# A hybrid decoder step on one core: residual through TensorE, a norm inside the dense stage, an embedding product beside the gathers

## The chip, the core and the metric

One Trainium2 chip, one of its cores. The metric is the device time of one execution in microseconds. The kernel is written instruction by instruction: each engine has its own program, and engines and DMAs wait for each other by semaphores that the code names. PE is TensorE, DVE is VectorE, ACT is ScalarE, POOL is GpSimd, SP is SyncE.

## What is computed

One layer of a decoder for 256 prompt tokens and 64 decode tokens (8 x 8), width 2048, all in float32. The part that matters here comes behind the attention:

```python
h = layer_norm(DEEPNORM_ALPHA * h + mixed, ln1_g, ln1_b)
h = layer_norm(DEEPNORM_ALPHA * h + peer_ffn(h, peer_wq, peer_subkeys, peer_u, peer_v), ln2_g, ln2_b)
gate = jax.nn.sigmoid(jnp.einsum('btd,de->bte', h, ple_gate))
return h + gate * jnp.einsum('btp,pd->btd', p_i, ple_proj)
...
def block(args):                      # of peer_ffn
    xt, et, gt = args                 # tokens, their 128 experts of 16384, gates
    u = u_tab[et]
    h = jnp.einsum('nd,nkd->nk', xt, u, preferred_element_type=jnp.float32)
    a = (gt * jax.nn.gelu(h, approximate=False)).astype(v_tab.dtype)
    return jnp.einsum('nk,nkd->nd', a, v_tab[et])
```

`p_i` has 256 columns; the product with `ple_proj` (256 x 2048) is called the embedding product below.

## The kernel before

Tokens lie on partitions in three tiles: tile 0 is decode (64 rows), tiles 1 and 2 are prompt (128 rows each). Large products take their float32 operands apart into a high part (made by ACT) and a low part (made by POOL for weights, by DVE for activations and V), and TensorE does three matmuls for each (`split_mm`, L1343).

- **Projections.** Weights come in pieces of 1 MB (`load_piece`, L340, two slots), of which ACT makes the high part (`hi`, L530), POOL the low part (`low`, L486). Pieces 0 to 79 are the input, output and query projections; 80 to 95 are the gate projection `ple_gate`, four column chunks of four pieces. `token_piece` (L1351) does a piece for the tiles given to it, 12 matmuls a tile.
- **Selection.** DVE picks each prompt token's experts: `select(t, c)` (L1162) for tile t and query chunk c, then `top_experts` (L1143) writes the expert numbers, which lets POOL start gathering. After `top_experts(0, 1)` DVE does `select(2, 1..3)` and `top_experts(1, 2)`, and then the dots.
- **Gathers and dots.** For each prompt tile and each of its 128 expert places POOL issues one indirect DMA that gathers 128 rows of `peer_u` (8 KB each) into a ring of 7 slots (L499 to L505); DVE multiplies it with the tokens and sums (`prompt_dot`, L1196). Among the dots of tile 2 stands the selection for the decode tokens (`after_dot`, L1229).
- **Gate matrix.** Prompt tokens do not gather `peer_v`. Their weights are put into a dense matrix of 256 tokens by 16384 experts: in 64 groups of four tokens, one-hot matrices of the two expert parts are multiplied on PE (`build`, L1595) into four PSUM banks in turn, and copied to SBUF (`build_copy`, by ACT at L707 and DVE at L1223). Groups 0 to 31 (tile 1) run beside the dots of tile 2; groups 32 to 63 behind them. ACT makes the one-hots of the first 32 and the second one-hots of most others (L678); DVE makes the first ones of groups 32 to 63 (L1208).
- **Dense stage.** 256 pieces of `peer_v` (half a MB each, five slots, loaded by SP at L457) are multiplied with the gate matrix, 12 matmuls a piece, into all eight banks (L1630 to L1641). ACT and DVE make the high and low parts. Between them DVE treats the decode tokens, packed on 128 partitions: 64 dots with gathered rows of `peer_u`, then 64 additions of gathered rows of `peer_v` (`decode_op`, L1254), at the pieces that the table `DECODE_AT` (L316 to L319) names; POOL issues a row when one before it is used.
- **Tail.** The tokens, which SP has written to the output tensor at L445 to make room, are read back at L461. DVE adds the sums from PSUM to them (`add_experts`, L1293), norms tile 1, 2 and 0 (`layer_norm`, L1043: statistics, variance, root by ACT, reciprocal, centring L1055, last step L1057), PE transposes them (`transposes`, L1330, banks by `T_LAST`), ACT and DVE make their parts, and the gate projection runs. Pieces 80 and 81 are done for tiles 1 and 2 first and for tile 0 later. Behind each of the pieces 82 to 93 stands one of the twelve parts of the embedding product (`ple_product`, L1666, plain float32). Sigmoid, product and sum per chunk, and four output DMAs follow.

SP's program is one queue: a wait in it holds back all loads behind it. The rest of the key-value cache copies stands between the loads.

## Time and profile before

| | |
|---|---|
| time, median of 3 runs | 2632.95 us (2630.96 to 2636.36) |
| the profiled execution's own time | 2637.14 us |
| its span, first to last instruction | 2635.3 us |
| PE busy | 1812.7 us, 69% |
| DVE busy | 1744.5 us, 66% |
| POOL busy | 1164.1 us, 44% |
| ACT busy | 867.1 us, 33% |
| moved by DMA | 880.83 MB, 334 GB/s over the span |
| PE clock granted, mean | 0.834 of full |

The page also draws the span in 40 slices: PE is busy at 7 to 9 tenths up to slice 13 and from slice 25 on, and nearly idle between; DVE and DMA are at 8 to 10 tenths in that gap. So the kernel has stages with different limits, and a busy share over the span tells of none of them. In a timeline a row is one instruction (or several alike, with their count), with its start and duration; brackets hold the idle time of the engine before it and what ended it. Matmuls are pipelined, and records of neighbours overlap.

### The profile page before, as it was taken

To read this page: it belongs to the slowest core of one execution; us is meant where nothing else is said; L and a number is where in the kernel's file an instruction comes from. 1 tells how busy PE (TensorE), PEld (TensorE's weight loads), DVE (VectorE), ACT (ScalarE), POOL (GpSimd) and SP (SyncE) were. 2 spreads that over 40 slices of the span, in tenths; PEclk is the share of its full clock that TensorE was granted. 3 is DMA by queue.
4 is the path that set the end of the run, shared out by engine and by line. 5 is a ranking of instruction groups with operands and counts; after the bars stand their busy time and mean duration, and the time that the engine had idled before them with its cause. 6 is when DMAs were issued, how large, how long until landed. Compare 5 with 4: busy or idle time off the path is not lost.

```text
span 2635.3 us, 25343 instructions
## 1 busy us (share of the span) xinstructions
PE 1812.7 (69%) x9670; PEld 1473.5 (56%) x9670; DVE 1744.5 (66%) x2409; ACT 867.1 (33%) x1359; POOL 1164.1 (44%) x484
## 2 busy tenths in 40 slices
PE   7998889999979400000120315999999999997698
PEld 6886778778769300000120314777777777775476
DVE  1054232521138899999999998888888999985321
ACT  2223222232222100000560984544444444443232
POOL 3553234335536148888767881122221222320343
PEclk9998899999989755555555557999999999998799
DMA  9997999978899349999999994799999999996345
GB/s 350 350 351 264 377 404 415 393 310 311 334 335 349 136 190 422 422 422 422 410 374 399 421 422 157 278 351 368 361 361 350 340 382 391 385 347 229 127 159 199
DMA packets 131399, 880.83 MB, mean 334 GB/s; under 512 B 18930, under 2 KB 20530, under 8 KB 55508
## 3 DMA queue, kind: packets, MB, share of 16 engines
q1 hardware_dynamic: 75988, 476.60, 47.3%
q0 software_dynamic: 55296, 402.68, 38.1%
q8 instruction: 74, 1.21, 0.2%
q14 instruction: 41, 0.34, 0.0%
HBM read 870.76 MB, written 141.11 MB: 384 GB/s over the span
## 4 chain that ended last, share of the span: by engine, by line
issue 29%; PE 22%; POOL 21%; DVE 16%; DMA 10%; ACT 1%; POOLq 0%; ACTq 0%; DVEq 0%
POOL expert_rows L504 14%; DMA v_raw<-in_peer_v 7%; PE psum L1347 7%; PE psum L1349 7%; PE psum L1348 7%; POOL w_lo L490 6%; DVE expert_rows L1200 5%; DMA expert_rows<-in_peer_u,experts 2%; DVE v_lo L1281 2%; DVE x_tokens L1269 2%; PE psum L1612 1%; ACT v_hi L753 1%; PE psum L1674 1%; DVE expert_rows L1260 1%; DVE chunk_one_hot L1140 1%
## 5 line engine op out<-in xcount | busy, mean ns | idle before, releaser
L504 POOL DMA_INDIRECT expert_rows<-in_peer_u,experts x256 | 523.1, 2043 | 189.0 <-DVE expert_rows L1200 83.3
L1200 DVE SCALAR_TENSOR_TENSOR expert_rows<-expert_rows,x_tokens 128x2048 f32<-128x2048 f32 x256 | 580.7, 2290 | 36.7 <-DMA expert_rows<-in_peer_u,experts 36.0
L490 POOL TENSOR_TENSOR w_lo<-w_raw,w_hi 128x2048 fp32r<-128x2048 f32 x80 | 373.3, 4667 | 500.5 <-ACT w_hi L535 500.5
L1347 PE MATMUL psum<-v_hi,gate_matrix_hi 128*128 128x512 f32 x1024 | 411.6, 402 | 28.9 <-DVE v_lo L1281 28.1
L753 ACT ACTIVATE v_hi<-v_raw 128x1024 fp32r<-128x1024 f32 x256 | 271.2, 1060 | 413.6 <-DMA v_raw<-in_peer_v 331.0
L1348 PE MATMUL psum<-v_lo,gate_matrix_hi 128*128 128x512 f32 x1024 | 405.5, 396 | 0.0
L1349 PE MATMUL psum<-v_hi,gate_matrix_lo 128*128 128x512 f32 x1024 | 405.2, 396 | 0.0
L1281 DVE TENSOR_TENSOR v_lo<-v_raw,v_hi 128x1024 fp32r<-128x1024 f32 x256 | 312.1, 1221 | 98.8 <-ACT v_hi L753 98.2
L535 ACT ACTIVATE w_hi<-w_raw 128x2048 fp32r<-128x2048 f32 x80 | 153.2, 1914 | 396.5 <-PE psum L1349 354.7
L1593 PE MATMUL psum<-identity,dots 128*128 128x128 f32 x2 | 0.9, 460 | 365.2 <-DVE row_max L1206 365.2
L1347 PEld LDWEIGHTS psum<-v_hi,gate_matrix_hi 128*128 128x128 f32 x1024 | 192.6, 188 | 99.3 <-DVE v_lo L1281 27.6
L1612 PE MATMUL psum<-one_hot_first_gated,one_hot_second 128*128 128x128 f32 x384 | 87.0, 400 | 227.2 <-ACT one_hot_first_gated L704 216.3
L512 POOL DMA_INDIRECT expert_rows<-in_peer_u,experts_decode x64 | 95.3, 1489 | 327.8 <-DVE expert_rows L1260 319.8
L1349 PEld LDWEIGHTS psum<-v_hi,gate_matrix_lo 128*128 128x128 f32 x1024 | 192.7, 188 | 47.1
L1348 PEld LDWEIGHTS psum<-v_lo,gate_matrix_hi 128*128 128x128 f32 x1024 | 192.9, 188 | 43.7
L1612 PEld LDWEIGHTS psum<-one_hot_first_gated,one_hot_second 128*128 128x128 f32 x384 | 75.3, 293 | 238.8 <-ACT one_hot_first_gated L704 219.7
L1347 PE MATMUL psum<-act_T_hi,w_hi 128*128 128x320 f32 x640 | 202.9, 317 | 7.0 <-DVE conv_z L870 2.0
L512 POOL DMA_INDIRECT expert_rows<-in_peer_v,experts_decode x64 | 96.2, 1504 | 249.8 <-DVE x_tokens L1269 229.5
L1593 PEld LDWEIGHTS psum<-identity,dots 128*128 128x128 f32 x2 | 0.4, 183 | 365.8 <-DVE row_max L1206 330.1
L1348 PE MATMUL psum<-act_T_lo,w_hi 128*128 128x320 f32 x640 | 199.9, 312 | 0.0
L1349 PE MATMUL psum<-act_T_hi,w_lo 128*128 128x320 f32 x640 | 199.8, 312 | 0.0
L1347 PE MATMUL psum<-w_hi,act_T_hi 128*128 128x512 f32 x480 | 188.9, 394 | 9.0 <-POOL w_lo L490 5.1
(273 smaller groups left out, 3255.1 us busy)
## 6 DMA issues: line engine op xcount, KB each, us to landing
v_raw<-in_peer_v SPq DMA_DIRECT2D x256, 512.0 KB, 7.3
out<-in_state_attn_k SPq DMA_DIRECT2D x64, 1020.0 KB, 9.8
out<-in_state_attn_v SPq DMA_DIRECT2D x64, 1020.0 KB, 10.0
w_raw<-in_w_in SPq DMA_DIRECT2D x48, 1024.0 KB, 7.9
cache_part<-in_k_parts SPq DMA_DIRECT2D x40, 1024.0 KB, 11.6
cache_part<-in_v_parts SPq DMA_DIRECT2D x40, 1024.0 KB, 13.5
w_raw<-in_w_out SPq DMA_DIRECT2D x16, 1024.0 KB, 5.2
w_raw<-in_peer_wq SPq DMA_DIRECT2D x16, 1024.0 KB, 6.3
```

What stands on the lines that cost most here:

```text
L490: nc.gpsimd.tensor_tensor(l_, r_, h_.bitcast(f32), ALU.subtract).then_inc(w_lo_ready, 1)
L504: pool.indirect_dma_start(ring[n % NSLOT][:, :], None, u_tab, bass.IndirectOffsetOnAxis(idx_p[:, n // PAIRS, n % PAIRS:n % PAIRS + 1], 0)) ...
L512: pool.indirect_dma_start(ring[i % DSLOT][:, :], None, u_tab if i < 64 else v_tab, bass.IndirectOffsetOnAxis(idx_d[:, i % 64:i % 64 + 1], ...
L535: A(bufs[1][:, slot, :, :], bufs[0][:, slot, :, :], ACT.Copy).then_inc(w_hi_ready, 1)
L753: A(vhi[m % HS][:, :], vrl[m % RL][:, :], ACT.Copy).then_inc(vh_ok, 1)
L1200: V.scalar_tensor_tensor(out=g, in0=g, scalar=1.0, in1=xt[:, t, :], op0=ALU.mult, op1=ALU.mult, accum_out=hdot[:, t, j:j + 1]).then_inc(u_ ...
L1269: V.scalar_tensor_tensor(out=ydec, in0=g, scalar=hdot[:, 0, i - 64:i - 63], in1=ydec, op0=ALU.mult, op1=ALU.add).then_inc(d_free, 1)
L1281: V.tensor_tensor(vlo[m % RL][:, :], vrl[m % RL][:, :], vhi[m % HS][:, :].bitcast(f32), ALU.subtract).then_inc(vl_d, 1)
L1347: MM(out, lh, rh, start=start, stop=False)
L1348: MM(out, lh, rl, start=False, stop=False)
L1349: return MM(out, ll, rh, start=False, stop=stop)
L1612: m = MM(PS[:, g % 4, j * NK:(j + 1) * NK], second_one_hot(g, j), emov[:, g % 2, j, :], start=True, stop=True)
```

## The change

1. The selections of tile 2 move in between the dots of tile 1: `select(2, 1)`, `(2, 2)`, `(2, 3)` and `top_experts(1, 2)` stand behind dots 8, 24, 40 and 56.
2. The embedding product runs as a whole between the two `part_transposes` on PE, its copies on ACT there too. Its result (`ple_out_early`, on the memory of the projections' weights) is written to the output tensors by SP, and read back into `ple_out` in the tail. The gate matrix, which takes the same memory, waits for that write.
3. The tokens of tiles 1 and 2 are scaled in place by ACT and brought by PE, with the identity, into the banks of the dense sums (`add_tokens`), so that the dense matmuls start with `start=False`. They are not written out and read back any more, and `add_experts` is gone. Tile 1's four banks are 0, 1, 4, 5 and take no builds now: groups 0 to 31 are built in banks 2, 3, 6, 7, groups 32 to 63 in banks 2 and 3 only. V slots 2, 3 and 4 lie elsewhere and are first loaded later.
4. `DECODE_AT`: the 64 dots stand 1.75 pieces apart (before 2), the 64 additions 1.875 (before 1.69), from piece 118 (before 134). The last is at piece 236. The fold of the decode sums, its gain and bias loads and its whole norm stand at pieces 242 to 253.
5. In the tail the statistics and the centring of tiles 1 and 2 read PSUM. The order of the tiles in the last projection is 0, 1, 2: piece 80 for tiles 0 and 1, transposes of tile 2, piece 81 for tiles 0 and 1, then both for tile 2.

```diff
-T_LAST = [(t, g, g + (0 if t else 4)) for t in (1, 2, 0) for g in range(4)]
+OUT_BANKS = ((0, 1, 4, 5), (2, 3, 6, 7))
+T_LAST = [(t, g, OUT_BANKS[t // 2][g]) for t in range(3) for g in range(4)]
+BUILD_BANKS = (2, 3, 6, 7)
...
-        U_AT = {2 * i: i for i in range(64)}
-        W_AT = {134 + (27 * i) // 16: 64 + i for i in range(64)}
-        GELU_AT = 130
+        U_AT = {(7 * i) // 4: i for i in range(64)}
+        W_AT = {118 + (15 * i) // 8: 64 + i for i in range(64)}
+        GELU_AT = 114
+        FOLD_AT = 242
+        ROOT_AT = 250
...
             sp.dma_start(xt[TS:128, 0, :], xt[0:TS, 0, :]).then_inc(pack_in, 16)
-            sp.dma_start(yp_v, xt[:, 1:3, :]).then_inc(spill, 16)
+            sp.wait_ge(w_lo_ready, 80)
+            sp.dma_start(plew[:, :, :], wple_v).then_inc(ple_in, 16)
+            sp.wait_ge(w_used, 80)
+            sp.dma_start(pnat[:, 1:3, :], pp_v).then_inc(ple_in, 16)
+            sp.dma_start(pnat[0:TS, 0, :], ps_v).then_inc(ple_in, 16)
+            sp.wait_ge(ple_ok, 12)
+            sp.dma_start(yp_v, ples[:, 1:3, :]).then_inc(ple_out, 16)
+            sp.dma_start(ys_v, ples[0:TS, 0, :]).then_inc(ple_out, 16)
...
                 if m == 0:
-                    sp.wait_ge(u_free, 128)
+                    sp.wait_ge(x_acc, 1)
                 if m == 2:
-                    sp.wait_ge(u_free, 256)
+                    sp.wait_ge(x_acc, 2)
+                if m == 3:
+                    sp.wait_ge(ab_mm, GROUPS)
                 if m == 4:
-                    sp.wait_ge(ab_mm, GROUPS)
+                    sp.wait_ge(x_acc, 3)
...
-                if m == 250:
+                if m == FOLD_AT:
                     sp.wait_ge(d_free, 128)
-                    sp.dma_start(xt2[0:TS, 0, :], ydec[TS:128, :]).then_inc(fold_in, 16)
-                    sp.dma_start(xt2[:, 1:3, :], yp_v).then_inc(x2_in, 16)
+                    sp.dma_start(xd2[0:TS, :], ydec[TS:128, :]).then_inc(fold_in, 16)
+                    sp.dma_start(ln2[:, 0, :], ln2_g.rearrange("a d -> (a d)").partition_broadcast(128)).then_inc(ln2_in, 16)
+                    sp.dma_start(ln2[:, 1, :], ln2_b.rearrange("a d -> (a d)").partition_broadcast(128)).then_inc(ln2_in, 16)
...
-            for c in range(1, 4):
-                select(2, c)
-            top_experts(1, 2)
...
-            after_dot = {1: {},
+            after_dot = {1: {8: lambda: select(2, 1), 24: lambda: select(2, 2), 40: lambda: select(2, 3),
+                             56: lambda: top_experts(1, 2)},
...
+            decode_norm = {243: decode_sums, 245: lambda: moments(0, decode_parts), 247: lambda: variance(0),
+                           251: decode_centre, 253: lambda: finish(0)}
...
+            sums = [[PS[:, b, :] for b in OUT_BANKS[t]] for t in range(2)]
+            moments(1, sums[0])
+            variance(1)
+            centre(4, 1, sums[0])
+            finish(1)
             transposed_lo(2, 0, 4)
+            moments(2, sums[1])
+            variance(2)
+            transposed_lo(2, 4, 8)
+            centre(5, 2, sums[1])
+            finish(2)
+            transposed_lo(2, 8, 12)
...
+            def add_tokens(t, cs):
+                for c in cs:
+                    m = MM(PS[:, OUT_BANKS[t - 1][c], :], ident[:, :], xt[:, t, c * CW:(c + 1) * CW], start=True, stop=False)
+                return m
...
-                if g >= 4:
-                    if by_dve(g - 4):
...
+                back = 4 if g < GROUPS // 2 + 2 else 2
+                if g >= back:
+                    evacuated(g - back)
...
+                if g == GROUPS // 2 + 3:
+                    pe.wait_ge(x_sc, 2)
+                    add_tokens(2, (2, 3)).then_inc(x_acc, 1)
...
             pe.wait_ge(tl_ready, 32)
-            for k in range(2):
-                token_piece(80 + k, k, 0, W_GATE, (1, 2))
+            token_piece(80, 0, 0, W_GATE, (0, 1))
             pe.wait_ge(ln_ok, 6)
             transposes(2, 8, 12)
+            token_piece(81, 1, 0, W_GATE, (0, 1))
             pe.wait_ge(tl_ready, 36)
             for k in range(2):
-                token_piece(80 + k, k, 0, W_GATE, (0,))
+                token_piece(80 + k, k, 0, W_GATE, (2,))
...
-                if p < 14:
-                    ple_product(p - 2)
```

**On DVE, behind the first table of experts.** `experts<-prompt_expert_part` is the table that lets the gathers start; the rows behind it are before:

```order
L1152 SCALAR_TENSOR_TENSOR experts<-prompt_expert_part 128x128
L1154 MEMSET row_max 128x1
L1155 MEMSET row_max 128x1
L1158 TENSOR_REDUCE cand_top<-gates 128x8
L1159 RECIPROCAL cand_top<-cand_top 128x8
L1160 TENSOR_TENSOR gates<-gates,cand_top 128x128
L1074 MAX chunk_top_values<-second_peer_scores 128x8 x4
L1077 MAX_INDEX chunk_top_keys<-chunk_top_values,second_peer_scores 128x8 x4
L1080 MATCH_REPLACE second_peer_scores<-chunk_top_values,second_peer_scores 128x128 x4
```

and now (line numbers of the changed kernel):

```order
L1178 SCALAR_TENSOR_TENSOR experts<-prompt_expert_part 128x128
...
L1186 TENSOR_TENSOR gates<-gates,cand_top 128x128
L1222 SCALAR_TENSOR_TENSOR expert_rows_98,dots<-expert_rows_98,x_tokens 128x2048
...
L1222 SCALAR_TENSOR_TENSOR expert_rows_99,dots<-expert_rows_99,x_tokens 128x2048
L1100 MAX chunk_top_values<-second_peer_scores 128x8 x4
L1103 MAX_INDEX chunk_top_keys<-chunk_top_values,second_peer_scores 128x8 x4
```

Before, three selections (the first begins at L1074) stand ahead of the first dot; now nine dots (L1222) come first, and the selection behind them.

**On DVE, behind the last low part of the dense stage.** Before, with `x_tokens_again` the tokens read back (the rows behind the first norm's last step repeat for the other tiles):

```order
L1288 TENSOR_TENSOR x_tokens_again<-x_tokens_again,x_tokens 64x2048
L1297 SCALAR_TENSOR_TENSOR x_tokens_again<-x_tokens_again,psum 128x512 x8
L1303 MEMSET row_max 128x1
L1048 BN_STATS ln_stats<-x_tokens_again 128x6 x4
L1050 BN_AGGR ln_mean_var<-ln_stats 128x2
...
L1055 SCALAR_TENSOR_TENSOR x_tokens_again<-x_tokens_again,ln_mean_var,ln_gain_bias 128x2048
L1057 SCALAR_TENSOR_TENSOR x_tokens_again<-x_tokens_again,ln_std,ln_gain_bias 128x2048
```

and now:

```order
L1300 BN_STATS ln_stats<-psum 128x6 x4
L1305 BN_AGGR ln_mean_var<-ln_stats 128x2
...
L1316 SCALAR_TENSOR_TENSOR prompt_out_tokens<-psum,ln_mean_var,ln_gain_bias 128x512 x4
L1320 MEMSET row_max 128x1
L1325 SCALAR_TENSOR_TENSOR prompt_out_tokens<-prompt_out_tokens,ln_std,ln_gain_bias 128x2048
L836 TENSOR_TENSOR out_T_lo<-psum,out_T_hi 128x4x64 x4
L1300 BN_STATS ln_stats<-psum 128x6 x4
```

The additions (L1297) are gone, the statistics and the centring read PSUM, and the low parts of the decode tile (L836) stand directly behind the first prompt tile's norm.

**On PE, from the query projection to the first build.** Before, the transposes of the two tables (L1588) and of the weights (L1593), and then the builds (L1612):

```order
L1563 MATMUL psum<-subkeys_T,peer_queries 64x128 x16
L1588 MATMUL psum<-identity,prompt_expert_part 128x128 x4
L1593 MATMUL psum<-identity,dots 128x128
L1612 MATMUL psum<-one_hot_first_gated,one_hot_second 128x128 x128
L1593 MATMUL psum<-identity,dots 128x128
```

and now:

```order
L1645 MATMUL psum<-identity,prompt_expert_part 128x128 x2
L1689 MATMUL psum<-identity,ple_tokens 128x64 x2
L1689 MATMUL psum<-identity,ple_tokens 128x128 x4
L1698 MATMUL psum<-ple_weights,ple_T 64x512 x2
L1698 MATMUL psum<-ple_weights,ple_T 128x512 x4
...
L1645 MATMUL psum<-identity,prompt_expert_part 128x128 x2
L1650 MATMUL psum<-identity,dots 128x128
L1660 MATMUL psum<-x_tokens,identity 128x512 x4
L1678 MATMUL psum<-one_hot_first_gated,one_hot_second 128x128 x128
```

The embedding product (L1689, L1698) stands between the two tables' transposes, and four products that bring in the scaled tokens (L1660) stand ahead of the first build.

## Rows read from the trace of the kernel before

**Rows 1.** Table of windows: stretch; busy us (instructions) of engines; clock, DMA share, GB/s
```profile
905.00:953.40 48.40, 1.22 (x4) 0.42 (x4) 46.13 (x188) 0.86 (x3) 6.99 (x7) 0.50 0.38 152
1100.00:1250.00 150.00, 0.00 (x0) 0.00 (x0) 137.90 (x119) 0.00 (x0) 129.67 (x61) 0.50 1.01 422
1267.70:1600.60 332.90, 66.89 (x257) 57.20 (x257) 317.04 (x372) 203.63 (x565) 252.28 (x126) 0.50 0.99 403
1600.60:1659.60 59.00, 40.97 (x257) 35.84 (x258) 43.19 (x154) 40.82 (x95) 0.70 (x1) 0.88 0.16 60
1659.60:2031.90 372.30, 365.50 (x1537) 286.97 (x1538) 325.72 (x322) 170.19 (x194) 92.87 (x64) 1.00 0.96 357
2031.90:2367.90 336.00, 321.94 (x1346) 248.79 (x1345) 306.17 (x236) 150.07 (x168) 91.82 (x61) 1.00 0.96 369
2373.47:2387.47 14.00, 14.00 (x62) 11.25 (x61) 7.43 (x8) 6.43 (x7) 0.00 (x0) 1.00 0.58 184
2367.90:2418.90 51.00, 46.73 (x193) 36.89 (x191) 24.53 (x24) 19.37 (x21) 0.00 (x0) 0.97 0.73 261
2418.90:2486.40 67.50, 28.14 (x127) 22.82 (x127) 38.50 (x51) 13.95 (x22) 16.16 (x4) 0.69 0.24 98
2486.40:2626.10 139.70, 139.70 (x552) 103.96 (x552) 20.49 (x18) 34.48 (x34) 59.77 (x13) 0.98 0.53 194
```

**Rows 2.** Chain of work that ended last: start us, us, what
```profile
137.13 4.60 POOL w_lo L490
...
153.45 4.60 POOL w_lo L490
...
1298.45 17.79 DVE expert_rows L1200 x16
```

**Rows 3.** Timeline of POOL: start, duration; in brackets the idle before
```profile
955.94 2.75 POOL L504 DMA_INDIRECT expert_rows<-in_peer_u,experts  x1 [42.12 <-DVE expert_rows L1200]
...
2437.34 11.60 POOL L490 TENSOR_TENSOR gate_w_lo<-gate_w_raw,gate_w_hi 128x2048 fp32r<-128x2048 f32 x2 [81.79 <-ACT gate_w_hi L535]
```

**Rows 4.** Timeline of VectorE, gathers: start us, duration us, line, operation, operands
```profile
910.98 0.20 DVE L1099 CAST chunk_top_keys_f<-chunk_top_keys 128x64 f32<-128x64 uint32 x1
...
926.37 0.20 DVE L1099 CAST chunk_top_keys_f<-chunk_top_keys 128x64 f32<-128x64 uint32 x1
...
953.37 2.29 DVE L1200 SCALAR_TENSOR_TENSOR expert_rows<-expert_rows,x_tokens 128x2048 f32<-128x2048 f32 x1
...
1090.18 2.29 DVE L1200 SCALAR_TENSOR_TENSOR expert_rows<-expert_rows,x_tokens 128x2048 f32<-128x2048 f32 x1 [0.18 <-DMA expert_rows<-in_peer_u,experts]
```

**Rows 5.** Timeline of PE, four places: end of builds, transposes, piece 82, product
```profile
1654.69 1.13 PE L1612 MATMUL psum<-one_hot_first_gated,one_hot_second 128*128 128x128 f32 x8 [0.28 <-issue]
...
2445.29 3.65 PE L1339 MATMUL psum<-identity,x_tokens_again 128*128 128x128 f32 x16 [9.27 <-DVE out_T_lo L810]
...
2486.39 0.79 PE L1347 MATMUL psum<-gate_w_hi,out_T_hi 128*128 128x512 f32 x1 [6.85 <-POOL gate_w_lo L490]
...
2607.88 1.88 PE L1674 MATMUL psum<-ple_weights,ple_T 128*128 128x512 f32 x4
```

**Rows 6.** Timeline of VectorE behind the dense stage
```profile
2418.90 4.99 DVE L1297 SCALAR_TENSOR_TENSOR x_tokens_again<-x_tokens_again,psum 128x512 f32<-128x512 f32 x8 [3.88 <-PE psum L1349]
...
2432.14 2.46 DVE L1048 BATCH_NORM_STATS2 ln_stats<-x_tokens_again 128x6 f32<-128x512 f32 x4
...
2435.68 2.35 DVE L1055 SCALAR_TENSOR_TENSOR x_tokens_again<-x_tokens_again,ln_mean_var,ln_gain_bias 128x2048 f32<-128x2048 f32 x1
2438.07 6.47 DVE L1057 SCALAR_TENSOR_TENSOR x_tokens_again<-x_tokens_again,ln_std,ln_gain_bias 128x2048 f32<-128x2048 f32 x1
...
2471.23 1.42 DVE L810 TENSOR_TENSOR out_T_lo<-psum,out_T_hi 128x256 fp32r<-128x256 f32 x4 [13.74 <-ACT out_T_hi L548]
```

**Rows 7.** Timeline of ACT: second gelu, and one high part
```profile
1600.66 0.31 ACT L666 ACTIVATE dots<-dots 128x128 f32<-128x128 f32 x1 [27.15 <-DVE row_max L1246]
...
2598.21 1.91 ACT L535 ACTIVATE gate_w_hi<-gate_w_raw 128x2048 fp32r<-128x2048 f32 x1 [6.45 <-PE psum L1349]
```

210 lines of the change are left out of this document (121 added, 89 removed).

## The prediction, made before the changed kernel was timed

> **What bounds the kernel now.** I read the table of windows first, because the kernel is a row of stages with different limits, then the timelines at the borders between stages. Shares over the whole span would say nothing here.
>
> [rows 1] is that table. From 905 to 1600.6 us the prompt tokens' expert rows are gathered and dotted; a window inside it shows DMA at 1.01 and 422 GB/s, so a gathered block of 128 rows of 8 KB, 1.049 MB, takes 1.049 / 422 GB/s = 2.485 us. VectorE's dots follow each other by 2.22 us when their rows are there already: 16 records are 8 dots with their accumulator reads, in 17.79 us [rows 2]. So DMA bounds this stage by a small margin, except where VectorE has other work. Ahead of it lies a hole: in 905 to 953.4 the DMA share is 0.38. POOL has issued seven gathers, which fill the ring of seven slots, and waits 42.12 us for the first dot [rows 3]. That dot starts at 953.37, because VectorE first does three selections, 15.39 us apart [rows 4].
>
> From 1600.6 to 1659.6 the second half of the gate matrix is built by TensorE, ScalarE and VectorE in a tight loop. From 1659.6 to 2418.9 TensorE bounds the dense product: a clean stretch does 5 pieces in 14.00 us, 2.80 each, at the full granted clock. The stage takes 759.3 us for 256 pieces, 42.5 above 716.8: 13.9 in pieces 0 to 127, 22.4 in 128 to 239, 6.2 in the last 16 (each stretch of [rows 1] less its pieces times 2.80).
>
> The tail is two things. From 2418.9 to 2486.4 VectorE's norms and the transposes stand in front of TensorE, whose clock is granted at 0.69. From 2486.4 to 2626.1 TensorE does the last fourteen pieces of the gate projection, with a part of the embedding product behind each of the first twelve.
>
> **Part 1: the embedding product leaves the last projection.** One of its twelve parts is four records over 1.88 us [rows 5]; the records overlap their neighbours, so I count 1.72 of it as TensorE's own. Is it TensorE that bounds a piece once the product is gone? A piece of the first projection has the same 36 matmuls and the same high and low parts, and two of them take 153.45 - 137.13 = 16.32 us [rows 2], 8.16 each. The stretch of 139.7 us is 14 x 8.16 + 12 x 1.72 and 4.8 for the ramp and the joins. So 12 x 1.72 = **-20.6 us**. In its new place TensorE is idle and ScalarE is busy 0.86 of 48.4 us [rows 1]. At the clock of 0.50 its 24 products take 24 x 0.86 x 2 = 41 us and are over by about 950. SP's queue is empty of other work there. The 2.6 MB written are 6 us of DMA, in a stretch where part 3 finds DMA idle. The read back of as much lies in a tail that moves under half of the 422 GB/s. Cost: nothing.
>
> **Part 2: the norms.** Before, VectorE's first instruction after the last dense matmul stands at 2418.90 [rows 6] and piece 82 starts at 2486.39 [rows 5]: 67.5 us. After, counted from that first instruction: four statistics of the sums in PSUM take 2.5 (as four from SBUF do), and 1.1 us later (2434.60 to 2435.68 in [rows 6]: variance, ScalarE's root, reciprocal) the centring starts, at 3.6. Four centrings from PSUM at 0.62 (eight such instructions took 4.99) end at 6.1. The norm's last step I take at 6.47 us, not at 2.35: the one of 2438.07 [rows 6] lay under POOL's low parts [rows 3], and ScalarE makes their high parts at the same point now. It ends at 12.6. Decode's low parts (1.4), the second tile's statistics (2.5) and variance (0.5) take VectorE to 17.0; beside them the first tile's sixteen transposes (3.65, [rows 5]) end at 16.8, and its low parts at 19.5. TensorE runs piece 80 for two tiles (5.6, and 1.5 for a slow start) to 26.7, the last tile's transposes to 30.4, piece 81 for two tiles to 36.0, and both pieces for the third tile to 41.6. The high part (1.91, [rows 7]) and low part (4.60) of piece 82 wait for piece 80 to be through, at 38.8: piece 82 starts at 45.5. Saved: 67.5 - 45.5 = **-22 us**. The 5.0 us of additions and the decode tile's norm, some 8 us, are in it. The decode norm now stands at pieces 243 to 253, 9.6 us of VectorE work where VectorE is busy 24.5 of 51.0 us [rows 1]: hidden by TensorE's pieces, and without that cover 9.6 us dearer.
>
> The Trainium skill (SBUF — State Buffer, "Who interferes with whom") says that VectorE and GpSimd share a port pair under an exclusive lock: a VectorE instruction with two SBUF inputs holds or waits for it, and issue order decides who waits. By that rule the 6.47 us were 2.35 of work behind a low part; if the step came first, by the 0.7 us that lie between the two, the tail would give 26 and the sum 2581. The trace agrees with a wait of that length in [rows 3, 6] and does not show the other order.
>
> **Part 3: selections between the dots.** The first dot comes at about 910.5 instead of 953.37. Nine dots at DMA's 2.485 end at 932.9; three selections (46.2), 48 dots at 2.22 (106.6) and 1.3 for the second table of experts bring dot 57 to 1087.0, against 1090.18 before [rows 4]: -3. But its ring is full now. Before, the full ring at the first dot let 57 dots pass in 136.8 us, 4.8 less than DMA's pace of 141.6. Together -8; a count of all 256 rows by the same rules gives -12. I take **-10 us**. It is far from 43, since VectorE, not DMA, bounds the first 57 dots: the wait for VectorE is cut up, not removed. Bounds: 0, and -33 (all that DMA stood idle).
>
> **Part 4: the scaled tokens through TensorE, and the build.** Scaling a tile is about 1.9 us of ScalarE; the first lies in its chain of one-hots, which ends 27.15 us before it is needed [rows 7], the second beside VectorE's first one-hots. Four products of 512 columns at 0.86, 7 us at the half clock, go ahead of the first build and under ScalarE's first one-hots. In the second half two products come into a loop where TensorE is busy 1.13 us a group of matmuls [rows 5]: +1.7. Two banks instead of four make a build wait for the copy of the group two before it, which in the last sixteen groups ScalarE does behind a one-hot: half a group on some six of them, +3. The last two products lie beside the last copy and the first V piece. **+5 us**, bounds 0 and 12.
>
> **Part 5: the dense stage.** Decode rows come every 1.75 pieces (before 2), then every 1.875 (before 1.69). With 0.524 MB a piece and 1.049 MB a row, the demand at 2.80 us a piece was 375 GB/s and then 409; it becomes 401, then 387. The stalls were 0.109 and 0.200 us a piece; on the line between them 401 gives 0.18 and 387 gives 0.14. 112 x 0.18 + 120 x 0.14 = 37, and 6 at the end, where again 2.5 MB go ahead of V pieces: 43 against 42.5. **0 us**. Bounds: -11 (0.109 everywhere) and +19 (0.2 everywhere, and the decode norm bare).
>
> **The sum**: -20.6 - 22 - 10 + 5 + 0 = -47.6. The profiled execution took 2637.14 us (span 2635.3), 4.2 above the median of 2632.95; the sum puts it at 2589.5, and the median at 2585.3.
>
> **Rivals.** (a) *The dense stage pays for the closer rows.* For it: 401 GB/s are asked for where 357 were moved. Against: 409 were asked for later, at 0.2 us a piece. +19: 2604. (b) *The gathers gain their whole hole*, if the selections slip into VectorE's waits for rows: -33 for -10, 2562. Against it: 57 dots and three selections are 173 us of VectorE work, their rows 142. (c) *The last projection does not reach 8.16*, because the chain of load, high and low part sets the piece once the product is gone: +10, 2595. The first projection speaks against it. (d) *Slower than before.* Late rows open gaps in the dense stage and TensorE's clock is granted at its lower level, 1.2 instead of 2.4 GHz; a piece then takes up to 5.6 us, +2.8. It decides from 17 such pieces on; 35 of them are +98, 2683. The last 16 pieces, with 6 us of gaps, took the clock to 0.97 only, and the 1.00 of the rest speaks against it. (e) *The gathers gain nothing*, if the product's copies on ScalarE or its DMAs hold up the second table of experts or the rows: +10, 2595.
>
> **How the numbers follow.** My forecast has 0.66, (a) 0.12, (b) 0.06, (c) 0.08, (e) 0.05, (d) 0.03. The forecast's own terms spread it by about 10 each way. The range goes down to 2567, part of the way to (b), and up to 2604 for (a). About 0.2% (5 us) is what a measurement can tell from no change. All but (d) are faster by more; 0.01 of (d) and 0.01 of bad ends together land within it: faster 0.95, same 0.02, slower 0.03.
>
> **What would show it.** First dot near 911, dot 57 near 1087; last dot near 1591; 64 us from there to the first dense matmul; 759 for the dense stage; 45.5 from VectorE's first instruction behind it to piece 82; then 119 us of TensorE. The forecast is wrong if the dense stage is over 775, or if pieces of the last projection stay above 9 us.

## The result, and where the time went

Over four runs of each the changed kernel took **2572.51 us** (2562.90 to 2576.15) against 2632.73 us for the kernel before: a ratio of **0.9759, 95% interval 0.9741 to 0.9777**, or 60.2 us less. The forecast for the median was 2585.3 us, 47.6 less, with a range from 2567 to 2604. A second set of runs gave 2576.69 us and a ratio of 0.9764 (0.9723 to 0.9805).

The profiled execution took 2572.92 us with a span of 2571.1. The table of windows of the changed kernel, cut at the same events as [rows 1] (stretch; length; busy us of PE, PEld, VectorE, ScalarE, POOL; granted clock, DMA share, GB/s):

```profile
906.70:1592.50 685.80, 97.81 (x323) 67.41 (x322) 652.18 (x815) 215.96 (x585) 520.72 (x259) 0.52 0.97 399
1592.50:1655.10 62.60, 45.64 (x266) 39.22 (x266) 42.90 (x155) 42.70 (x96) 0.81 (x1) 0.83 0.14 50
1655.10:2034.00 378.90, 360.78 (x1547) 287.24 (x1548) 343.67 (x333) 171.77 (x195) 88.59 (x70) 1.00 0.97 370
2034.00:2354.00 320.00, 310.94 (x1344) 249.87 (x1343) 290.09 (x227) 148.71 (x168) 79.87 (x55) 1.00 0.97 367
2354.00:2402.10 48.10, 43.63 (x185) 35.35 (x183) 29.55 (x32) 18.93 (x22) 0.00 (x0) 0.96 0.65 239
2402.10:2445.80 43.70, 26.64 (x122) 22.15 (x121) 25.63 (x39) 13.71 (x18) 15.68 (x4) 0.77 0.37 138
2445.80:2561.80 116.00, 116.00 (x504) 95.62 (x504) 19.05 (x18) 28.72 (x22) 59.55 (x13) 0.99 0.62 229
```

Three things stand out against [rows 1]. The stretch that began at 905 with a DMA share of 0.38 is no stretch of its own any more: from the first gather to the last dot the mean share is 0.97 (0.95 before). It is not even: it is 0.97 in the first 46.7 us, but 0.87 from 953.4 to 1100, where the kernel before had 0.97. Part of the hole has moved behind the first dots. The stretch of the norms is 43.7 us instead of 67.5, and the last one 116.0 instead of 139.7, with 504 matmuls instead of 552: the 48 of the embedding product are gone. And the first half of the dense stage shows **PE busy 360.78 us for 1547 matmuls**, where the kernel before had 365.50 for 1537. The same matmuls have become cheaper, and no part of the change does that on purpose.

The timelines give the borders exactly. Both kernels measured from start to start of the named instructions:

| stretch | before | after | change | forecast |
|---|---|---|---|---|
| span's start to the first gather | 904.99 | 906.67 | +1.7 | 0 |
| first gather to last dot | 693.21 | 683.53 | -9.7 | -10 |
| last dot to first dense matmul | 61.41 | 64.88 | +3.5 | +5 |
| first to last dense matmul | 758.86 | 746.63 | **-12.2** | 0 |
| last dense matmul to piece 82 | 67.92 | 44.03 | -23.9 | -22 |
| piece 82 to the last matmul | 139.35 | 115.77 | -23.6 | -20.6 |
| last matmul to the end | 9.6 | 9.6 | 0.0 | 0 |

The sum is -64.2 between two profiled executions, against -47.6. A good 12 of the 16.6 us that the forecast missed lie in the dense stage, for which it had forecast nothing.

Two matmuls of the same kind in the timeline of PE in the changed kernel, twelve records (one piece) apart in a stretch without a stall (start, duration):

```profile
2339.80 0.39 PE L1404 MATMUL psum<-v_hi,gate_matrix_hi 128*128 128x512 f32 x1
...
2342.52 0.39 PE L1404 MATMUL psum<-v_hi,gate_matrix_hi 128*128 128x512 f32 x1
```

A piece is 2.72 us, where the clean stretch of [rows 1] has five pieces in 14.00, 2.80 each. At a granted clock of 1.00 in both, a matmul follows the last by 0.2267 instead of 0.2333 us. Over 256 pieces that is 20.5 us, of which stalls took back 8: they grew from 42 to 50 us.

### The profile page after: what moved, and what is told of

Its sections match the earlier page's. It is cut to its first block, busy times and chain, and to the rows that moved or that the text cites. A ratio compares the mean times of both kernels' runs of the same rounds, so it can differ in the third digit from the quotient of the medians.

```text
span 2571.1 us, 25379 instructions
## 1 busy us (share of the span) xinstructions
PE 1804.6 (70%) x9686; PEld 1480.7 (58%) x9686; DVE 1733.0 (67%) x2408; ACT 872.7 (34%) x1361; POOL 1138.8 (44%) x484
## 4 chain that ended last, share of the span: by engine, by line
PE 46%; DVE 23%; POOL 12%; DMA 11%; issue 6%; ACT 2%; SPq 0%; ACTq 0%; DVEq 0%; POOLq 0%
PE psum L1404 14%; PE psum L1406 13%; PE psum L1405 13%; POOL expert_rows L523 11%; DVE expert_rows L1222 9%; DMA v_raw<-in_peer_v 7%; DVE v_lo L1348 2%; DMA cache_part<-in_k_parts 2%; DMA expert_rows<-in_peer_u,experts 2%; DVE expert_rows L1283 2%; PE psum L1558 1%; DVE x_tokens L1292 1%; PE psum L1523 1%; ACT v_hi L793 1%; PE psum L1678 1%
## 5 line engine op out<-in xcount | busy, mean ns | idle before, releaser
L1222 DVE SCALAR_TENSOR_TENSOR expert_rows<-expert_rows,x_tokens 128x2048 f32<-128x2048 f32 x256 | 577.8, 2289 | 30.7 <-DMA expert_rows<-in_peer_u,experts 29.7
L523 POOL DMA_INDIRECT expert_rows<-in_peer_u,experts x256 | 514.7, 2011 | 187.7 <-DVE expert_rows L1222 81.4
L1404 PE MATMUL psum<-v_hi,gate_matrix_hi 128*128 128x512 f32 x1024 | 405.9, 396 | 33.5 <-DVE v_lo L1348 33.1
L1405 PE MATMUL psum<-v_lo,gate_matrix_hi 128*128 128x512 f32 x1024 | 399.7, 390 | 0.0
L1406 PE MATMUL psum<-v_hi,gate_matrix_lo 128*128 128x512 f32 x1024 | 399.5, 390 | 0.0
L531 POOL DMA_INDIRECT expert_rows<-in_peer_u,experts_decode x64 | 82.9, 1296 | 304.1 <-DVE expert_rows L1283 296.1
L1405 PE MATMUL psum<-w_lo,act_T_hi 128*128 128x512 f32 x480 | 188.5, 393 | 0.0
L1406 PE MATMUL psum<-w_hi,act_T_lo 128*128 128x512 f32 x480 | 188.4, 393 | 0.0
```

The costliest lines, as they stand in the source:

```text
L523: pool.indirect_dma_start(ring[n % NSLOT][:, :], None, u_tab, bass.IndirectOffsetOnAxis(idx_p[:, n // PAIRS, n % PAIRS:n % PAIRS + 1], 0)) ...
L531: pool.indirect_dma_start(ring[i % DSLOT][:, :], None, u_tab if i < 64 else v_tab, bass.IndirectOffsetOnAxis(idx_d[:, i % 64:i % 64 + 1], ...
L1222: V.scalar_tensor_tensor(out=g, in0=g, scalar=1.0, in1=xt[:, t, :], op0=ALU.mult, op1=ALU.mult, accum_out=hdot[:, t, j:j + 1]).then_inc(u_ ...
L1404: MM(out, lh, rh, start=start, stop=False)
L1405: MM(out, lh, rl, start=False, stop=False)
L1406: return MM(out, ll, rh, start=False, stop=stop)
```

## What the experiments were to decide

The new statistics tile `ln2_mean_var` takes 32 bytes ahead of `gate_matrix_hi` and `gate_matrix_lo`, the two tiles that every dense matmul reads. The high tile starts at 222592 instead of 222560, the low one at 225664 instead of 225632. Theory: the start sets the pace. Rivals: the new table of decode rows, or the shape of the stage around the matmuls. Beyond that each term of the sum was to be isolated, because two terms that came out near their forecast may have done so by chance.

## Experiments on the dense stage

**The kernel before, with 32 bytes ahead of the two tiles.**

```diff
+    off[0] += 32
     ghs = small("gate_matrix_hi", [128, ST, 2 * 128], f32r, 4)
     gls = small("gate_matrix_lo", [128, ST, 2 * 128], f32r, 4)
```

> The kernel before with 32 unused bytes ahead of the two small tiles gate_matrix_hi and gate_matrix_lo, which start 32 bytes off a multiple of 64 there and on one in the changed kernel; nothing else differs. In the dense stage a piece without a stall takes 2.80 us before and 2.72 in the changed kernel. Theory A (the tiles' start address sets it): 2.72 us here, 256 x 0.08 = 20 us less, of which more stalls take back up to 8: 2613 to 2620 us. Theory B (it comes from matmuls that add to sums already in the banks, or from the V slots' places, or from the row table): 2.80 us and no change, 2633 us.

Measured: 2629.48 us, ratio 0.9972 (0.9952 to 0.9991), a piece 2.72 us. The whole dense stage in its table of windows:

```profile
1659.80:2412.10 752.30, 719.99 (x3072) 571.03 (x3072) 656.04 (x580) 338.79 (x383) 187.14 (x125) 1.00 0.94 359
```

With nothing else touched (no other tile lies behind these two) the pace of the changed kernel is there: its cause is the place of the tiles. But the time fell by 7 us and not by 20. PE is busy 719.99 us and the stage takes 752.30. Above 256 clean pieces the stage has 56 us of stalls, where the kernel before had 42.

**The changed kernel, with the same 32 bytes**, so that the tiles start at 222624 and 225696.

```diff
+    off[0] += 32
     ghs = small("gate_matrix_hi", [128, ST, 2 * 128], f32r, 4)
```

> The changed kernel with the same 32 bytes ahead of gate_matrix_hi, which puts both tiles where they are off a multiple of 64, as before. Theory A: a piece without a stall takes 2.80 us again, and the time rises by 12 to 20 us, to 2585 to 2592. Theory B: 2.72 us and no change, 2572 us.

Measured: 2579.46 us, ratio 0.9795 (0.9771 to 0.9820), a piece 2.80 us again. The time rose by less than the 12 to 20 us expected.

```profile
1651.90:2407.20 755.30, 728.86 (x3072) 572.53 (x3072) 664.06 (x591) 339.48 (x384) 167.97 (x125) 1.00 0.94 356
```

**The changed kernel, with the 32 bytes ahead of the low tile alone.**

```diff
     ghs = small("gate_matrix_hi", [128, ST, 2 * 128], f32r, 4)
+    off[0] += 32
     gls = small("gate_matrix_lo", [128, ST, 2 * 128], f32r, 4)
```

> The changed kernel with the 32 bytes between the two tiles, so that only gate_matrix_lo is off a multiple of 64. It is the stationary operand of one matmul in three. If the stationary operand's address costs each matmul that loads it (theory A1), a piece takes 2.72 + 0.08 / 3 = 2.75 us and the time rises by 4 to 7 us; if VectorE's or ScalarE's writes beside it are what costs (A2), it may be anything from 0 to 20 us.

Measured: 2583.34 us, ratio 0.9818 (0.9794 to 0.9843), a piece 2.80 us. Only one matmul in three reads the low tile, and yet the piece lost all it had gained. The mean intervals between starts, over all of the stage that ran without a pause, show how: 0.2326 us from the first matmul to the second, both of which read the high tile, 0.2381 to the third, which reads the low one, and 0.2289 to the next first. In the changed kernel the three are 0.2275, 0.2275 and 0.2276. Reading the displaced tile costs most, and the interval between the two matmuls that do not read it has grown as well.

**The changed kernel, with the tiles 64 bytes up** (222656), to tell whether a start that is 32 past a multiple of 64 was the point.

```diff
+    off[0] += 64
     ghs = small("gate_matrix_hi", [128, ST, 2 * 128], f32r, 4)
```

> The changed kernel with the gate matrix's two tiles moved up by 64 bytes, so that their start stays a multiple of 64; it is the control to the move by 32. Theory A (what slows the dense matmuls is a start that is 32 past a multiple of 64): 2.72 us a piece, time as the changed kernel's, 2570 to 2578. Theory B (any move away from the one address, or the one tile's distance to others, sets it): 2.80 us a piece, 2579 or more.

Measured: 2584.54 us, ratio 0.9812 (0.9792 to 0.9833), a piece 2.80 us.

```profile
1653.80:2408.20 754.40, 732.17 (x3072) 574.29 (x3072) 663.56 (x591) 340.30 (x384) 167.37 (x125) 1.00 0.94 357
```

So no multiple of 64 decides: my reading after the first three runs fell here.

**The tiles 128 bytes up** (222720), together with an edit of the tail that is told below.

```diff
+    off[0] += 128
     ghs = small("gate_matrix_hi", [128, ST, 2 * 128], f32r, 4)
```

> The changed kernel with ScalarE's order in the tail turned as in the run before of that name, and with the gate matrix's two tiles moved up by 128 bytes, which changes nothing else. The high tile's start was 222592 in the changed kernel (2.72 us a piece of the dense stage), 222560 and 222624 (2.80) with 32 bytes less or more, and 222656 with 64 more (2.80), so it is no multiple of 64 that decides. Theory A (a multiple of 128 decides; 222592 is one, 222656 is none, 222720 is the next): 2.72 us a piece, piece 82 again 39 to 40 us behind VectorE's first instruction of the tail, and the whole as the run with the turned order, ratio to the kernel before 0.975 to 0.978. Theory B (the one address or the distance to other tiles decides): 2.80 us a piece and 7 to 10 us more, ratio 0.979 to 0.981.

Measured: 2574.87 us, ratio 0.9761 (0.9737 to 0.9784); a piece 2.78 to 2.80 us.

```profile
1659.50:2414.70 755.20, 729.78 (x3072) 576.75 (x3072) 664.29 (x591) 340.04 (x384) 164.51 (x125) 0.99 0.93 357
```

A multiple of 128 does not decide either. (A start 128 past a multiple of 256, or a distance to other tiles, is not ruled out.) What stands is narrower: of six placements one, 222592 with 225664, gives 2.72 us, in both kernels and in every version of them that kept it; the five others give 2.78 to 2.80. Why that one, the runs do not say.

At the slow pace this run was expected at a ratio of 0.979 to 0.981. It has 0.9761, where the same tail with the tiles at the fast place has 0.9762 (below). Between these two the pace makes no difference in time that can be measured; the other three moved versions, at 0.9795, 0.9812 and 0.9818, are 8 to 16 us behind the changed kernel.

**The changed kernel, with the decode table of the kernel before.**

```diff
-        U_AT = {(7 * i) // 4: i for i in range(64)}
-        W_AT = {118 + (15 * i) // 8: 64 + i for i in range(64)}
+        U_AT = {2 * i: i for i in range(64)}
+        W_AT = {134 + (27 * i) // 16: 64 + i for i in range(64)}
...
-        GELU_AT = 114
+        GELU_AT = 130
```

> The changed kernel with the decode table of before (dots each 2 pieces, additions each 1.69 from piece 134, gelu at 130). The dense stage of the changed kernel stalls 50 us over 256 pieces of 2.72. Theory of the prediction (the tables cost the same, stalls follow the bytes asked for on one line): the same within 4 us, 2572. Rival (the additions at 1.69 stall most, the new table is what gives the dense stage part of its gain): 8 to 16 us slower, 2580 to 2588, and the excess in pieces 134 to 240.

Measured: 2580.97 us, ratio 0.9808 (0.9785 to 0.9832). Its profiled execution, 2568.20 us, is the fastest of its four; there a piece is 2.72 us and the stage from first to last matmul 745.9, so the table is not what made the pieces faster. By the ratios the old table is 0.0044 to 0.0049 worse, 12 us; the profile shows no place for that, and the new table was not measured in the same set of runs. Whether the table gives anything stays open.

**The changed kernel unchanged, a second time**, beside the next three.

> The changed kernel as it is, run again beside the kernel before and beside the three below, because its time against a version of it with the old table of decode rows is to be read on one chip. Theory A (the 2572.5 us are the kernel's): 2568 to 2577, ratio to before 0.974 to 0.978, dense stage 745 to 748 at 2.72 us a piece. Theory B (the first measurement was a lucky one, and the two tables are the same): about 2580, ratio 0.980.

Measured: 2576.69 us (2570.03 to 2583.65). In its profiled execution, 2581.93 us, the dense stage takes 755.0 us at the same 2.72 a piece, where the first one took 746.6. **One execution's dense stage is uncertain by some 8 us**, and the term "-12.2" of the table above is partly that. Taken together (first to last dense matmul, one profiled execution each):

| | a piece | dense stage, us | mean |
|---|---|---|---|
| kernel before and three variants (below) | 2.80 | 758.9, 752.0, 753.4, 756.2 | 755.1 |
| kernel before, 32 bytes | 2.72 | 752.0 | 752.0 |
| changed kernel moved, four variants | 2.78 to 2.80 | 755.0, 756.7, 754.2, 754.9 | 755.2 |
| changed kernel, twice, and three variants | 2.72 | 746.6, 755.0, 748.5, 749.2, 745.9 | 749.2 |

At an equal pace the stage is the same in both kernels, 755.1 and 755.2 us, between executions that scatter by several us: the closer decode rows cost nothing that shows. The faster matmuls are worth 3 to 6 us of the stage by these means, not 20.5. Where did the rest go? One limit is DMA: its share is 0.97 in the two long windows of the changed kernel (0.96 before), and the chain of work that ended last goes, in this stage, again and again through loads of V (start, us):

```profile
1944.23 10.29 DMA v_raw<-in_peer_v
2016.08 8.91 DMA v_raw<-in_peer_v
2042.65 7.77 DMA v_raw<-in_peer_v
2070.28 8.98 DMA v_raw<-in_peer_v
2090.89 8.64 DMA v_raw<-in_peer_v
2149.04 10.32 DMA v_raw<-in_peer_v
```

The pieces of V and the decode rows alone are 268 MB (256 of 0.524 and 128 of 1.049 MB); at the 369 GB/s of these windows they take 727 us, an estimate that leaves a faster TensorE little room.

But VectorE is in the loop too, and the pauses end with it. It makes the low part of every piece and does the decode tokens' work between; by the table of windows it is busy 663.31 of the stage's 747.0 us, 2.59 us a piece. One pause of the changed kernel, piece 44, in the timelines of ScalarE, VectorE and PE:

```profile
1780.43 1.06 ACT L793 ACTIVATE v_hi<-v_raw 128x1024 fp32r<-128x1024 f32 x1 [0.22 <-DMA v_raw<-in_peer_v]
...
1781.02 2.28 DVE L1283 SCALAR_TENSOR_TENSOR expert_rows<-expert_rows,x_tokens 128x2048 f32<-128x2048 f32 x1
...
1783.23 0.61 DVE L1346 TENSOR_TENSOR gate_matrix_lo<-gate_matrix,gate_matrix_hi 128x256 fp32r<-128x256 f32 x1
...
1783.76 1.22 DVE L1348 TENSOR_TENSOR v_lo<-v_raw,v_hi 128x1024 fp32r<-128x1024 f32 x1
...
1785.12 0.47 PE L1404 MATMUL psum<-v_hi,gate_matrix_hi 128*128 128x512 f32 x1 [0.94 <-DVE v_lo L1348]
```

The high part was ready at 1781.49, and VectorE, at work without a pause since 1776.53, began the low part at 1783.76. Counted so over the stage, the pauses of over 0.05 us between pieces are 40 us in the changed kernel, and 29 of them stand before pieces whose high part had been ready for over 0.15 us; before the rest the high part itself came late. In the kernel before it is 20 of 34. Most of these unbroken runs of VectorE begin with a low part that had waited for its load, so the two limits cannot be told apart from this. What is shown is that TensorE, the loads into five slots, ScalarE and VectorE stand in one loop with little slack anywhere. Which of DMA's rate, the five slots and VectorE's work takes back the faster matmuls, no run separates: a version with a sixth slot, or with the decode work off VectorE, was not tried.

## Experiments on the gathers and the build

**The changed kernel, with its selections ahead of the dots again.**

```diff
+            for c in range(1, 4):
+                select(2, c)
+            top_experts(1, 2)
...
-            after_dot = {1: {8: lambda: select(2, 1), 24: lambda: select(2, 2), 40: lambda: select(2, 3),
-                             56: lambda: top_experts(1, 2)},
+            after_dot = {1: {},
```

> The changed kernel with its three selections of the second tile of tokens and the second table of experts put back ahead of the prompt tokens' dots, nothing else. Theory A (the move of the selections alone gives the stage of the dots its 8 us, and nothing beside): the first dot near 955, dot 57 near 1092, the last dot 8 to 10 us later than 1590.2, the whole 2580 to 2584. Theory B (the stage is bound by DMA further on, and what the move gave at its start is lost to it later, so that the 8 us come from somewhere else): last dot within 3 us of 1590.2, the whole within 3 us of the changed kernel. Theory C (the whole hole of 43 us counts): last dot after 1620.

Measured: 2580.16 us, ratio 0.9784 (0.9751 to 0.9817). Its POOL and VectorE timelines, first gather and last dot:

```profile
906.24 1.08 POOL L523 DMA_INDIRECT expert_rows<-in_peer_u,experts  x1 [30.69 <-DVE row_max L1180]
```

```profile
1595.52 2.29 DVE L1225 SCALAR_TENSOR_TENSOR expert_rows<-expert_rows,x_tokens 128x2048 f32<-128x2048 f32 x1
```

The stage takes 689.3 us: 5.8 more than 683.5, and 3.9 less than the 693.2 of the kernel before. The move of the selections is worth 5.8 us, not 9.7, and less than the 8 to 10 expected here. The four profiles of the kernel before and its variants with nothing edited in this stage have 692.4 to 693.5 us, the eight of the changed kernel and its variants 682.4 to 683.9, so both differences are clear of the scatter. Side by side, this version and the kernel before run alike up to dot 128 but for 0.9 us, and part by 2.6 us between dots 128 and 144. In the kernel before that stretch of VectorE's timeline reads:

```profile
1273.28 2.29 DVE L1200 SCALAR_TENSOR_TENSOR expert_rows<-expert_rows,x_tokens 128x2048 f32<-128x2048 f32 x1 [0.76 <-DMA expert_rows<-in_peer_u,experts]
1277.06 2.29 DVE L1200 SCALAR_TENSOR_TENSOR expert_rows<-expert_rows,x_tokens 128x2048 f32<-128x2048 f32 x1 [1.47 <-DMA expert_rows<-in_peer_u,experts]
1280.17 2.29 DVE L1200 SCALAR_TENSOR_TENSOR expert_rows<-expert_rows,x_tokens 128x2048 f32<-128x2048 f32 x1 [0.81 <-DMA expert_rows<-in_peer_u,experts]
```

Rows come 3 to 4 us apart instead of 2.49. Just ahead SP had issued two loads of V, which waited for dot 128; in the changed kernel they wait for the products that bring in the tokens scaled by ScalarE, and go 16.7 us later (SP's timeline, the kernel before, then the changed kernel):

```profile
1267.56 0.81 SPq L457 DMA_DIRECT2D v_raw<-in_peer_v  x2
```

```profile
1284.28 0.82 SPq L479 DMA_DIRECT2D v_raw<-in_peer_v  x2
```

**The kernel before, with these two loads behind dot 138.**

```diff
-                    sp.wait_ge(u_free, 128)
+                    sp.wait_ge(u_free, 138)
```

> The kernel before, with the loads of the first two pieces of V issued behind dot 138 and not behind dot 128 of the prompt tokens; in the changed kernel they wait for the scaling of the tokens, which falls there as well. Theory A (at dot 128 rows are bound by DMA, and the two loads, 1.05 MB, put 2.5 us ahead of the next rows; ten dots on VectorE is busy with the decode selections and they cost nothing): from the first gather to the last dot 690.4 to 691 us instead of 693.2, the whole 2 to 3 us down. Theory B (the loads cost the same wherever they stand): 693 again; the 3.9 us that the changed kernel gains there beside its selections come from elsewhere.

Measured: 2631.01 us, ratio 0.9985 (0.9966 to 1.0003), which as a time is no proof. The stage, read from its timelines, is: first gather at 904.62, last dot at

```profile
1594.78 2.29 DVE L1200 SCALAR_TENSOR_TENSOR expert_rows<-expert_rows,x_tokens 128x2048 f32<-128x2048 f32 x1 [0.17 <-DMA expert_rows<-in_peer_u,experts]
```

That is 690.2 us, 3.0 less than 693.2. But this execution is 1.0 ahead at dot 128 already, where nothing was edited. What the edit does stands behind it: dots 128 to 144 take 43.7 us instead of 46.3, as they do in the changed kernel (43.7), and 46.3 in the three other variants of the kernel before, which leave the loads where they were. The same bytes cost 2.6 us where rows are bound by DMA, and nothing 29 us later (1296.89), where VectorE does decode selections between its dots. So of the stage's 9.7 us, 5.8 are the selections and 2.6 V's first loads; the remaining 1.3 are within the scatter, for the profile of the kernel before is 0.5 to 1.0 behind its four variants at dot 128.

**The kernel before, with the second half of the builds over two banks.**

```diff
+        def build_bank(g):
+            return g % 4 if g < GROUPS // 2 else g % 2
...
+                back = 4 if g < GROUPS // 2 + 2 else 2
+                if g >= back:
...
-                    m = MM(PS[:, g % 4, j * NK:(j + 1) * NK], second_one_hot(g, j), emov[:, g % 2, j, :], start=True, stop=True)
+                    m = MM(PS[:, build_bank(g), j * NK:(j + 1) * NK], second_one_hot(g, j), emov[:, g % 2, j, :], start=True, stop=True)
```

> The kernel before with the gate matrix's second half built over two banks of PSUM instead of four, as the change does it, and nothing else. Theory A (a build waits for the copy of the group two ahead of it): from the last dot to the first dense matmul 64 to 65 us instead of 61.4, and the whole 3 us up. Theory B (ScalarE and VectorE set the pace and two banks are enough): within 1 us of 61.4. Theory C (every group waits): 67 or more.

Measured: 2641.61 us, ratio 1.0013 (0.9992 to 1.0034). From the last dot (1602.23) to the first dense matmul (1666.00) it takes 63.8 us instead of 61.4: **+2.4**, which would leave 1.1 of the 3.5 for the two products of the scaled tokens in the loop. Neither is exact: this stretch takes 61.4 to 62.9 us in the kernel before and its three variants without this edit, and 64.5 to 66.2 in the changed kernel and its variants.

## Experiments on the tail

**The kernel before, without the embedding product**: the twelve parts behind pieces 84 to 95 and their copies are left out, and VectorE multiplies the gate by other data of the same shape, so the output is another.

```diff
-                if p >= 4:
-                    ple_copy(p - 4)
...
-                dve.wait_ge(ple_ok, 3 * c + 3)
...
-                    m = V.tensor_tensor(gsig[0:r, t, :], gsig[0:r, t, :], pleo[0:r, t, cc], ALU.mult)
+                    m = V.tensor_tensor(gsig[0:r, t, :], gsig[0:r, t, :], plew[0:r, 0, cc], ALU.mult)
...
-                if p < 14:
-                    ple_product(p - 2)
```

> The kernel before without the embedding product: the twelve parts that stand behind pieces 84 to 95, their copies by ScalarE and VectorE's wait for them are gone, and the gate is multiplied by the layer norm's weights in its place, so that VectorE's instruction keeps its shape; the output is another. Theory A (each part is 1.72 us of TensorE's own, as the prediction has it): the last stretch falls from 139.7 us by 20.6, its pieces take 8.16 each, the whole comes to 2610 to 2614 beside 2633. Theory B (the new tail's gain of 23.7 in this stretch is the product alone): 139.7 falls by 23 or more, to 116. Theory C (the product lay partly in waits that remain): the fall is under 15.

Measured: 2615.65 us, ratio 0.9923 (0.9902 to 0.9944). The start of piece 82 and the last matmul in PE's timeline:

```profile
2486.53 0.80 PE L1344 MATMUL psum<-gate_w_hi,out_T_hi 128*128 128x512 f32 x1 [6.85 <-POOL gate_w_lo L490]
...
2603.32 0.39 PE L1346 MATMUL psum<-gate_w_hi,out_T_lo 128*128 128x512 f32 x1
```

116.8 us instead of 139.35: **22.6 us for twelve parts, 1.88 each**, which is the full record of [rows 5] and not the 1.72 that I counted.

**The changed kernel, with piece 80's high part behind VectorE's norm step.** In the changed kernel VectorE's timeline behind the dense stage is:

```profile
2402.14 2.49 DVE L1300 BATCH_NORM_STATS2 ln_stats<-psum 128x6 f32<-128x512 f32 x4 [5.84 <-PE psum L1406]
...
2405.71 2.73 DVE L1316 SCALAR_TENSOR_TENSOR prompt_out_tokens<-psum,ln_mean_var,ln_gain_bias 128x512 f32<-128x512 f32 x4
2408.48 5.55 DVE L1325 SCALAR_TENSOR_TENSOR prompt_out_tokens<-prompt_out_tokens,ln_std,ln_gain_bias 128x2048 f32<-128x2048 f32 x1
...
2423.62 2.35 DVE L1325 SCALAR_TENSOR_TENSOR prompt_out_tokens<-prompt_out_tokens,ln_std,ln_gain_bias 128x2048 f32<-128x2048 f32 x1
```

and POOL's:

```profile
2407.36 11.06 POOL L509 TENSOR_TENSOR gate_w_lo<-gate_w_raw,gate_w_hi 128x2048 fp32r<-128x2048 f32 x2 [79.77 <-ACT gate_w_hi L554]
```

The same instruction takes 5.55 us under the low parts and 2.35 without. POOL had begun 1.1 us earlier, and the chain of waits puts the border between its two low parts at 2411.85: from 2408.48 that is 3.37 us, and the remaining 2.18 are about the instruction itself. The second low part, behind the step, then took 6.57 us:

```profile
2411.85 6.57 POOL gate_w_lo L509
```

```diff
+            transposed_hi(2, 0, 4)
+            act.wait_ge(ln_ok, 5)
...
+            transposed_hi(2, 4, 8)
...
-            transposed_hi(2, 0, 8)
```

> The changed kernel with one order of ScalarE's turned in the tail: it makes the first half of the second tile's high parts, then waits for VectorE's last norm step of the first prompt tile, and only then makes piece 80's high part, whose low part GpSimd takes up. No work is added or taken away. In the changed kernel that step of VectorE took 5.55 us under GpSimd's low parts, and 2.35 us without them elsewhere. Theory A (two engines share a lock, and whoever issues first holds it): the step takes 2.35 us, piece 82 starts 40 to 41 us after VectorE's first instruction of the tail instead of 43.6, the whole is 3 us under the changed kernel, 2569 to 2574 on a chip where that takes 2572 to 2577. Theory B (the step is slowed by DMA or PSUM traffic and not by GpSimd): it still takes over 4.5 us and the time is unchanged. Theory C (the low part of piece 80 or 81 comes too late now): the step is short, but TensorE waits at piece 80, 81 or 82 for it, and the time is unchanged or worse.

Measured: 2572.59 us, ratio 0.9762 (0.9743 to 0.9781). The timelines of this version, VectorE:

```profile
2400.53 2.49 DVE L1302 BATCH_NORM_STATS2 ln_stats<-psum 128x6 f32<-128x512 f32 x4 [5.84 <-PE psum L1408]
...
2406.87 2.35 DVE L1327 SCALAR_TENSOR_TENSOR prompt_out_tokens<-prompt_out_tokens,ln_std,ln_gain_bias 128x2048 f32<-128x2048 f32 x1
...
2418.86 3.73 DVE L1327 SCALAR_TENSOR_TENSOR prompt_out_tokens<-prompt_out_tokens,ln_std,ln_gain_bias 128x2048 f32<-128x2048 f32 x1
```

POOL:

```profile
2411.34 9.10 POOL L509 TENSOR_TENSOR gate_w_lo<-gate_w_raw,gate_w_hi 128x2048 fp32r<-128x2048 f32 x2 [84.88 <-ACT gate_w_hi L554]
```

and PE, piece 82:

```profile
2439.73 0.80 PE L1406 MATMUL psum<-gate_w_hi,out_T_hi 128*128 128x512 f32 x1 [3.93 <-POOL gate_w_lo L509]
```

The step is 2.35 us now, and the low parts, which no such step interrupts until they are through, take 9.10 for two instead of 11.06. The second tile's step begins at 2418.86, 1.58 us before they end (2420.44), and takes 3.73. Whoever came first held the other up, in either direction: the steps at 2408.48 and 2418.86 waited for a low part under way, and the second low part of the changed kernel, behind a step, took 6.57 us where two undisturbed ones take 9.10. The Trainium skill (SBUF — State Buffer, "Who interferes with whom") describes it so, and this trace now agrees with it in both orders. Piece 82 starts 39.2 us behind VectorE's first instruction instead of 43.6 (40 to 41 was expected). That is **4.4 us less tail, but not a measurably faster kernel**: 0.9762 beside 0.9759 and 0.9764, with intervals of 0.2 to 0.4% each way. The run with the tiles 128 bytes up holds the same edit, with 40.4 us from VectorE's first instruction (2414.88) to piece 82 (2455.26), and the ratio of 0.9761 already given. A gain of 4.4 us is under what these runs can tell by time alone, and no version tried here is measurably better than the changed kernel.

## Why the prediction was right, and what was off

**Part 1, the product (-20.6; measured -23.6).** The mechanism stands: pieces take 8.16 us without it, and its new place costs nothing (its last copy by ScalarE is at 933.67 us; 950 was forecast). The price was mis-sized. I took 1.72 of the 1.88 us, reasoning that the records overlap their neighbours; alone it measured 1.88, 1.9 us in all. The last 1.0 is the ramp: piece 82 takes 9.91 us in the changed kernel, from its first matmul to that of the next piece, and 10.93 in the kernel before without the product. TensorE idled less ahead of it (clock 0.77 in the stretch instead of 0.69), and eight intervals between its matmuls are at the slow 0.43 us instead of twelve. In its new place the product was faster than forecast: I had the clock stay at 0.50 and the matmuls take 41 us; they took 24.49, from 909.14 on, at a granted clock of 0.90.

```profile
2445.74 0.50 PE L1404 MATMUL psum<-gate_w_hi,out_T_hi 128*128 128x512 f32 x1 [3.94 <-POOL gate_w_lo L509]
```

**Part 2, the norms (-22; measured -23.9).** From VectorE's first instruction to piece 82 it takes 43.6 us; 45.5 was forecast. The norm's last step was taken at 6.47 and measured 5.55. The choice of the long value over 2.35 was right, and for the reason given; the other order was then worth 4.4 us, where the sentence on it had 4 (26 for 22). The rest of this part, the additions that are gone and the decode norm that has moved, is read off the two timelines; no run isolates it.

**Part 3, the gathers (-10; measured -9.7).** The number was right and the account was not. By my steps the selections alone gave 8, which I rounded up to 10 by a count of all rows; they gave 5.8: 1.7 at dot 57 and nearly all the rest by dot 128. From 953.4 to 1100, where VectorE does two of the three selections, DMA's share is only 0.87. The missing part was an edit that I had costed at nothing: the first two loads of V now wait for the scaled tokens instead of dot 128, which gave 2.6. That the two and some scatter came to the rounded 10 is luck. I had asked what the scaling delays, and not that a delay can move bytes out of a stretch bound by DMA. Dot 57 came at 1089.30 (1087 forecast), the last at 1590.20 (1591).

**Part 4, the build (+5; measured +3.5).** Two banks cost 2.4 (3 forecast), which leaves 1.1 for the products in the loop (1.7), each within 1.5 us of scatter.

**Part 5, the dense stage (0; measured -12.2).** This is the step that failed, in two ways. First, "TensorE bounds the dense product" held only for the clean pieces; with DMA at 0.96 to 0.97, as [rows 1] already showed, and VectorE at 2.6 us a piece, the stage has no single limit. The forecast put the stalls down to the bytes asked for alone, where most of them stand behind work of VectorE's. Second, the sum took 2.80 us a piece as given, while the change displaced the operands by 32 bytes and made it 2.72. That is worth 3 to 6 us by the means of the stage. By the ratios it is nothing in one pair (0.9761 and 0.9762), 7 us in another (0.9972 for the shift alone) and 8 to 16 in the rest (0.9795 to 0.9818 against 0.9759 and 0.9764), so its size is not settled. What is left of the 12.2 is the scatter of single executions: 758.9 is the longest of the kernel before with its variants, 746.6 nearly the shortest of the other group. At the old pace the forecast of 0 holds within that scatter. With 6 us for the shift the terms give -9.7 + 3.5 - 6 - 23.9 - 23.6 = -59.7, or -58.0 with the 1.7 us ahead of the first gather, against 60.2 measured between medians; each term has the scatter of one execution, so the closeness proves little.

**The rivals.** (a) fell: the closer rows cost nothing that shows at an equal pace, and 19 us would. (b) fell: VectorE does bound the first dots, and the hole of 43 us gave 5.8. (c) fell with 8.16 us a piece, (d) with a granted clock of 1.00 in the stage, (e) with the -9.7.

## What to carry to other kernels

A small tile added anywhere moves everything allocated behind it: compare the pace of a matmul between two builds before explaining a stage by its schedule, and try the hot operands at a few placements. Where several engines and DMA are all near full in one loop, a faster one gives back only the little slack of the others; their busy time for each round of the loop, read in that window, warns of it in advance. And when an edit makes a transfer wait for something new, ask from which stretch its bytes leave and into which they go, not only who is delayed.
